# Block products in two interleaved halves of columns: a three-level read and write pattern on the matmuls of one large float32 kernel

## What is computed

```python
for l in range(DEPTH):                      # DEPTH = 2
    h = modulate(x, g_norm[l, 0], mod[:, 0], mod[:, 1])
    x = x + 0.5 * mod[:, 2][:, None, :] * swiglu(h, w_ffn1_gu[l], w_ffn1_down[l])
    h = modulate(x, g_norm[l, 1], mod[:, 3], mod[:, 4])
    x = x + mod[:, 5][:, None, :] * hybrid_mixer(h, w_in[l], w_out[l], ...)
    h = modulate(x, g_norm[l, 2], mod[:, 6], mod[:, 7])
    x = x + 0.5 * mod[:, 8][:, None, :] * swiglu(h, w_ffn2_gu[l], w_ffn2_down[l])
```

## Time and profile before

| what | value |
|---|---|
| median of three runs | 2960.03 us |
| the profiled execution, its own time | 2960.58 us |
| its span, first to last instruction | 2958.8 us |
| TensorE busy with matmuls | 2814.6 us, 95% of the span |
| mean granted TensorE clock | 0.972 |
| VectorE, GpSimd, ScalarE busy | 1459.2, 1136.2, 1012.2 us |
| bytes read from HBM | 364.04 MB |

### The profile page before, as it was taken

The page is one execution under the profiler, slowest core; times in us unless marked ns, Lnnn a source line. Parts: engine busy times, 40 slices in busy tenths (PEclk is TensorE's granted clock), DMA queues, the critical chain, the costliest instruction groups (busy, mean ns, idle before and its releaser), DMA issues.

```text
span 2958.8 us, 37062 instructions
## 1 busy us (share of the span) xinstructions
PE 2814.6 (95%) x13036; PEld 2288.0 (77%) x13036; DVE 1459.2 (49%) x2627; ACT 1012.2 (34%) x1449; POOL 1136.2 (38%) x488
## 2 busy tenths in 40 slices
PE   7999999999999999999989999988889999999997
PEld 4888877778888788887768888877666778788886
DVE  3525365554435543445745253654654555473645
ACT  2222235432222322224533222344444553243322
POOL 2444443234444444444233444453310323344433
PEclk9999999999999999999999999988999999999998
DMA  6535342135344354443214353632200114322221
GB/s 242 200 141 183 130 171 86 58 117 183 135 163 171 144 185 155 170 144 141 72 72 149 136 180 143 230 132 86 93 29 15 66 53 148 112 96 90 99 100 43
DMA packets 69269, 374.37 MB, mean 127 GB/s; under 512 B 7776, under 2 KB 8544, under 8 KB 38656
## 3 DMA queue, kind: packets, MB, share of 16 engines
q1 hardware_dynamic: 65424, 359.61, 33.9%
q10 hardware_dynamic: 3696, 12.85, 1.1%
HBM read 364.04 MB, written 8.39 MB: 126 GB/s over the span
## 4 chain that ended last, share of the span: by engine, by line
PE 37%; issue 32%; POOL 20%; DVE 4%; ACT 2%; DMA 1%; ACTq 1%; DVEq 1%; SPq 1%; POOLq 0%
POOL w_lo L407 20%; PE psum L472 9%; PE psum L473 9%; PE psum L474 9%; PE psum L878 2%; PE psum L900 1%; PE psum L491 1%; PE psum L493 1%; PE psum L492 1%; PE psum L888 1%; DVE psum L1918 1%; ACT w_hi L992 0%; PE psum L528 0%; SPq L368 0%; DMA raw<-in_weights_dram 0%
## 5 line engine op out<-in xcount | busy, mean ns | idle before, releaser
L407 POOL TENSOR_TENSOR w_lo<-raw,w_hi 128x1024 fp32r<-128x1024 f32 x464 | 1115.1, 2409 | 1664.3 <-ACT w_hi L992 1664.2
L472 PE MATMUL psum<-h_hi,w_hi 128*128 128x512 f32 x2080 | 820.6, 395 | 17.3 <-DVE h_lo L1437 16.6
L473 PE MATMUL psum<-h_lo,w_hi 128*128 128x512 f32 x2080 | 816.4, 392 | 0.0
L474 PE MATMUL psum<-h_hi,w_lo 128*128 128x512 f32 x2080 | 815.6, 392 | 0.0
L992 ACT CAST w_hi<-raw 128x1024 fp32r<-128x1024 f32 x464 | 482.5, 1049 | 886.7 <-PE psum L474 726.3
L472 PEld LDWEIGHTS psum<-h_hi,w_hi 128*128 128x128 f32 x2080 | 395.3, 190 | 104.6 <-DVE h_lo L1437 15.8
L473 PEld LDWEIGHTS psum<-h_lo,w_hi 128*128 128x128 f32 x2080 | 395.4, 190 | 82.4 <-issue 0.5
L474 PEld LDWEIGHTS psum<-h_hi,w_lo 128*128 128x128 f32 x2080 | 394.8, 190 | 83.0
L472 PE MATMUL psum<-hid_hi,w_hi 128*128 128x512 f32 x880 | 343.4, 390 | 5.5 <-DVE hid_lo L1924 5.5
L473 PE MATMUL psum<-hid_lo,w_hi 128*128 128x512 f32 x880 | 343.1, 390 | 0.0
L474 PE MATMUL psum<-hid_hi,w_lo 128*128 128x512 f32 x880 | 342.9, 390 | 0.0
(11 more groups left out here) (348 smaller groups left out, 3135.6 us busy)
## 6 DMA issues: line engine op xcount, KB each, us to landing
raw<-in_weights_dram SPq DMA_DIRECT2D x232, 1024.0 KB, 5.6
mod_raw<-in_mod_w_dram SPq DMA_DIRECT2D x192, 512.0 KB, 4.0
first_mods_a<-in_mod_w_dram SPq DMA_DIRECT2D x8, 512.0 KB, 11.9
first_mods_b<-in_mod_w_dram SPq DMA_DIRECT2D x8, 512.0 KB, 15.4
first_mods_a<-gate_spill ACTq DMA_DIRECT2D x4, 1024.0 KB, 12.1
gate_spill<-gate_out_c ACTq DMA_DIRECT2D x5, 512.0 KB, 3.0
x<-in_xT_dram SPq DMA_DIRECT2D x1, 2048.0 KB, 8.6
x_spill<-x ACTq DMA_DIRECT2D x1, 2048.0 KB, 12.6
```

The lines of the kernel that those rows point to most:

```text
L407: pool.tensor_tensor(w_lo[:, k % 2, cs], raw[:, k % 4, cs], w_hi[:, k % 2, cs].bitcast(F32), ALU.subtract).then_inc(lo_ready, 1)
L472: pe.matmul(out, wh, rhs_hi[:, c, :], start=(c == ks[0]), stop=False)
L473: pe.matmul(out, wh, rhs_lo[:, c, :], start=False, stop=False)
L474: mm = pe.matmul(out, wl, rhs_hi[:, c, :], start=False, stop=(c == ks[-1]))
```

## The change

A helper `lines` regroups the columns of an operand: its free dimension of `2 * b * 16` columns is read as two halves (`a`) of `b` groups of 16 neighbouring columns (`c`), and walked with `b` outermost, then `a`, then `c`. For 512 columns the walk is 0 to 15, 256 to 271, 16 to 31, 272 to 287 and so on: 32 runs of 16 columns (64 bytes). For 256 columns it is 16 runs with halves of 128. Moving operand and output are walked alike, so each result lands at the address it had before. The number of instructions, the weights, the waits and everything outside `products` stay.

```diff
+            def lines(ap):
+
+                return ap.rearrange("p (a b c) -> p b a c", a=2, c=16)
+
             def products(g, k, rhs, ks=range(KC), waits=None, width=T, between=None, half=False):
...
-                    out = psum[:, 2 * (k % 2) + t, 0:width]
-                    pe.matmul(out, wh, rhs_hi[:, c, :], start=(c == ks[0]), stop=False)
-                    pe.matmul(out, wh, rhs_lo[:, c, :], start=False, stop=False)
-                    mm = pe.matmul(out, wl, rhs_hi[:, c, :], start=False, stop=(c == ks[-1]))
+                    out = lines(psum[:, 2 * (k % 2) + t, 0:width])
+                    hi, lo = lines(rhs_hi[:, c, :]), lines(rhs_lo[:, c, :])
+                    pe.matmul(out, wh, hi, start=(c == ks[0]), stop=False)
+                    pe.matmul(out, wh, lo, start=False, stop=False)
+                    mm = pe.matmul(out, wl, hi, start=False, stop=(c == ks[-1]))
```

## The result

The changed kernel takes 3076.06 us (median of four runs, 3073.2 to 3077.75) where the kernel before takes 2960.28 us in the same comparison: ratio 1.039, 95% interval 1.0375 to 1.0404. It is 116 us slower. The forecast was 2960; the rival "a cycle lost at each jump" had said 3077.

A forecast was written before the change was run, and what follows sets the result against it. The prediction took TensorE's own pace to bound the kernel. Instructions, levels and jumps were priced 0 + 0 + 0 on the profiled 2960.58 us, giving a forecast of 2960.0 us, range 2954 to 3085.

The forecast's parts named there:

- a cycle lost at each jump: Lines 472 to 474, moving reads or PSUM writes: 0.417 ns a jump, 116.5 us, about 3077 us; chance of slower 0.27.
- TensorE's pace is the bound, and nothing absorbs a change of it: Whole kernel: TensorE busy 2814.6 of 2958.8 us, so a change of its pace enters the time nearly undiminished.
- Counts and distances: Lines 472 to 474: 8880 wide matmuls 0.2267 us apart, 288 narrow 0.1200 us; together 2048 us, 69% of the span.
- More levels in the pattern, taken as 0: Touched matmul instructions: three levels instead of one; longer preparation would hide under the matmul before, price 0.
- The jumps, taken as 0: Lines 472 to 474: 279,600 jumps between runs, priced 0 from VectorE's rows at line 1918; the term called deciding.
- No reserve to hide a stumble: Argument for the slower rival: TensorE's rows show one column at every single cycle, hence nothing to hide a loss.
- The 32 cycles beside the columns: Each touched matmul: a fixed 13.3 ns whatever its width, looking like the change of weights, which the pattern leaves alone.
- The rival's mechanism: Moving reads or PSUM writes: where the address leaves a run, the array gets no column for one cycle, 0.417 ns.
- The skill's rule: PSUM: any non-contiguous pattern slows matmuls significantly, size not given; a second form makes runs of 16 harmless.

The follow-up runs named there:

- Write-only: The changed kernel with only the output walked in interleaved halves and the moving operand read unbroken; 2960.64 us, ratio 0.9996 to the kernel before.
- two_levels: Against the changed kernel, the moving operand is its first 16 columns read 32 times (narrow matmuls: 8 columns), output written unbroken; 3086.2 us, one run.
- near: Against the changed kernel, neighbouring runs of 16 columns lie 128 bytes apart instead of 1 KiB, on both operands; 3076.33 us, ratio 1.0389.

## Why the prediction was wrong, point by point

The measured 3076.06 us lies inside the range of 2954 to 3085 only because the range had been stretched over the nearer rival; the forecast itself was no change, and the distance of the wide matmuls moved by 13.3 ns where 0.7 was to show it wrong.

- **TensorE's pace is the bound, and nothing absorbs a change of it**: right. The span grew by 114.0 us where TensorE's busy time grew by 117.5, with the same waits.
- **Counts and distances** (8880 and 288; 0.2267 and 0.1200 us): right, and they are why the rival's sum hit: 8880 x 13.3 ns.
- **More levels in the pattern, taken as 0**: right. Write-only has three levels on the output and costs 0.9996 of the time, and runs of 64 have three on the moving operand too and stand at 226.7 ns.
- **The jumps, taken as 0: the step that failed.** They cost 13.3 ns a wide matmul, 115.7 us on the steps at full clock. I took the value from the row I called nearest, VectorE's runs of 63 columns. Two things were wrong in that choice. VectorE takes a column every 1.02 ns, and TensorE itself, slowed to 0.83 ns a column, pays nothing either (0.427 us before and after); a supply that suffices at that pace says nothing of the pace of 0.417 ns. And the runs there are 63 columns long, where TensorE's aligned 64-column runs are free as well. The row measured neither the rate nor the length in question. I had named the first weakness and then gave it 27%.
- **"No reserve to hide a stumble"**, the argument for the rival, was the better reading of the earlier trace rows: an engine that gets a column in every cycle has nothing left for a gap.
- **The 32 cycles beside the columns**: read as the change of weights, "whatever its width". Wrong: the rows at the lower clock in the same trace, which I did not read, show 512 cycles and nothing beside, and two_levels cut them to 12 on the narrow matmuls. That they are supply as well is likely, not shown. The equal 32 at both widths had looked like proof.
- **The rival's mechanism** was right in one of its two places (the moving read) and, by luck, in its size at this point (12.9 against 13.3 ns), and wrong in its law: not a cycle a jump, no price on PSUM writes, none on the narrow matmuls with 16 runs (6.3 ns forecast), none for 3 or 7 jumps.
- **The skill's rule.** The Trainium skill, page "PSUM — Partial Sum Buffer", section "Specifications (TRN2)", has any non-contiguous PSUM pattern slow matmuls significantly. The write-only run is against it for runs of 16 columns (0.9996); the narrower form in "Advanced Engine Details and Errata", section "PSUM Cachelines", with two consecutive elements, agrees with it. For reads, the Trainium skill, page "Advanced Engine Details and Errata", section "SBUF Cachelines", has accesses to the same 16-byte line at full performance and asks for at least two hits on a line to absorb the memory's latency. Aligned runs of 4 to 32 columns meet that and still cost 9.9 to 23.4 ns here, so for these matmuls at full clock it is not enough.

**What stays open** is what the supply does at a short run. That the price starts between 64 and 32 columns, counts the alignment of a run and does not add up by jumps would fit a reader that fetches aligned pieces ahead of the array and falls behind when too many are left half used; this was argued, not shown. Only one misaligned walk was tried, with starts 224 bytes apart, so the grain of the alignment is not known. Why narrow matmuls keep 0.120 us with 16 runs, and why the steps of near alternate, was not tried.

## What to carry to other kernels

Read a moving float32 operand of 512 columns in unbroken stretches of at least 64 that start at a multiple of 64 columns (256 bytes), the shortest that was free here; put any regrouping of columns on the PSUM side, where 16-column runs were free. Before taking a price of zero from another engine's row, compare the pace: a row at 1 ns a column cannot vouch for one at 0.4 ns. And look for the same instruction at both granted clocks: what vanishes at the lower one is not the array's work but something that runs beside it.

## What the runs showed of the hardware that was not expected

- Wide fp32r matmuls stand 512 / 2.4 + 13.3 = 226.7 ns apart at full clock and 512 / 1.2 = 427 ns at half clock, unbroken or in runs down to 4 columns.
- Short runs in the moving read cost 9.9, 13.3, 16.7 and 23.4 ns a wide matmul for runs of 32, 16, 8 and 4 columns; 64 and 128 cost nothing, and 64 that start every 56 columns 6.7 ns.
- Narrow matmuls reading the same 8 columns 32 times stand 111.7 ns apart, closer than unbroken ones (120.0) and than those whose 32 runs of 8 lie apart (123.3).
- Loading 64 instead of 128 weight columns, or one column 128 times, made unbroken wide matmuls slower (230 and 231 ns against 226.7), not faster.
